# Moving the second expert item's first product ahead of the first item's down product

## The reference, cut to what matters

```python
gate = ...                      # [256, 32], two experts of one group of eight per token
h = silu(einsum('td,edf->tef', t, w1)) * einsum('td,edf->tef', t, w3)   # f = 512
h = h * gate[:, :, None]
y = einsum('tef,efd->td', h, w2)
out = rmsnorm(h_in + y)
```

## Time and profile before

| | us |
|---|---|
| median of 3 runs | 1465.17 (1464.26 to 1465.79) |
| the profiled execution | 1466.02 |
| its span in the trace | 1463.5 |
| TensorE busy | 1382.6 (94%) |
| VectorE busy | 553.4 (38%) |
| ScalarE busy | 341.1 (23%) |
| 16 DMA engines, large queue | 78.2% of the span |

### The profile page before, as it was taken

One profiled execution on the slowest core, in us unless ns is written; L12 is line 12 of the kernel. 1 busy time (PEld: TensorE's weight loads), 2 busy tenths in 40 slices (PEclk: granted clock), 3 DMA queues, 4 the chain that ended last, 5 costly groups with the idle time before them and its releaser, 6 DMA issues.

```text
span 1463.5 us, 19372 instructions
## 1 busy us (share of the span) xinstructions
PE 1382.6 (94%) x7304; PEld 784.6 (54%) x7304; DVE 553.4 (38%) x1103; ACT 341.1 (23%) x608; POOL 206.9 (14%) x195
## 2 busy tenths in 40 slices
PE   6999899998999999998999999899999999899896
PEld 5874698896687435433533543444534543443354
DVE  4899710424534423322313223223222332321345
ACT  3010158565565011110111111111121020121102
POOL 2000356676584000000000000000000000000000
PEclk9999999999999999999999999999999999999996
DMA  8433443344357599999999999959999999999991
GB/s 208 172 116 115 144 173 126 127 151 172 115 195 322 223 426 428 428 428 428 427 428 427 429 429 429 429 222 430 429 427 429 429 429 428 427 430 429 428 403 58
DMA packets 71374, 471.67 MB, mean 322 GB/s; under 512 B 17297, under 2 KB 17378, under 8 KB 46114
## 3 DMA queue, kind: packets, MB, share of 16 engines
q1 hardware_dynamic: 70674, 469.75, 78.2%
q10 hardware_dynamic: 528, 1.05, 0.2%
q0 software_dynamic: 128, 0.26, 0.1%
HBM read 468.95 MB, written 2.10 MB: 322 GB/s over the span
## 4 chain that ended last, share of the span: by engine, by line
PE 61%; DMA 19%; DVE 3%; ACT 1%; issue 1%; DVEq 0%; POOL 0%; POOLq 0%; ACTq 0%
PE ps L1767 24%; DMA ring<-in_expert_w_dram 19%; PE ps L1428 11%; PE ps L1785 11%; PE ps L1745 5%; PE ps L1775 3%; PE ps L1796 2%; PE ps L1797 2%; PE ps L1757 1%; PE ps L1717 1%; DVE reg_e L1074 0%; PE ps L1693 0%; DVE reg_y L1036 0%; DVE reg_x L1371 0%; PE ps L1551 0%
## 5 line engine op out<-in xcount | busy, mean ns | idle before, releaser
L1785 PE MATMUL ps<-ring,reg_y 128*64 128x512 f32 x1056 | 240.5, 609 | 8.7 <-DVE reg_y L1293 7.8
L529 POOL TENSOR_TENSOR w_lo<-ring,w_hi 128x512 fp32r<-128x512 f32 x144 | 185.3, 1316 | 87.5 <-ACT w_hi L586 86.1
L1299 DVE TENSOR_TENSOR y_lo_t<-ps,y_hi_t 64x512 fp32r<-64x512 f32 x132 | 90.9, 689 | 216.6 <-ACT y_hi_t L812 215.3
L1785 PEld LDWEIGHTS ps<-ring,reg_y 128*64 128x64 f32 x1056 | 75.4, 140 | 147.3 <-issue 143.6
L812 ACT ACTIVATE y_hi_t<-ps 64x512 fp32r<-64x512 f32 x132 | 78.0, 591 | 327.3 <-PE ps L1785 324.9
L1308 DVE TENSOR_TENSOR reg_x<-ps,reg_x 128x512 f32<-128x512 f32 x136 | 87.7, 684 | 131.1 <-PE ps L1797 131.1
L1767 PE MATMUL ps<-reg_e,reg_s 128*64 128x512 f32 x528 | 119.4, 594 | 10.6 <-POOLq L551 10.6
L1767 PE MATMUL ps<-ring,reg_s 128*64 128x512 f32 x528 | 120.0, 596 | 7.7 <-POOLq L551 7.2
L1767 PE MATMUL ps<-ring,reg_y 128*64 128x512 f32 x528 | 120.0, 596 | 6.8 <-POOLq L551 6.2
L1767 PE MATMUL ps<-reg_e,reg_y 128*64 128x512 f32 x528 | 119.3, 594 | 2.2 <-POOLq L551 1.4
L1288 DVE TENSOR_SCALAR reg_y<-ps,lamv 128x512 f32<-128x512 f32 x33 | 24.8, 751 | 242.9 <-PE ps L1767 242.9
(11 more groups left out here) (360 smaller groups left out, 1763.9 us busy)
## 6 DMA issues: line engine op xcount, KB each, us to landing
ring<-in_expert_w_dram SPq DMA_DIRECT2D x128, 2048.0 KB, 20.3
reg_e<-in_expert_w_dram SPq DMA_DIRECT2D x64, 2048.0 KB, 20.5
ring<-in_w_in_dram SPq DMA_DIRECT2D x20, 2048.0 KB, 7.9
ring<-in_w_out_dram SPq DMA_DIRECT2D x8, 2048.0 KB, 8.0
reg_x<-in_x_dram SPq DMA_DIRECT2D x4, 1024.0 KB, 8.6
out_dram<-reg_x SPq DMA_DIRECT2D x4, 512.0 KB, 2.7
reg_e<-in_ssm_w_glu_dram ACTq DMA_DIRECT2D x1, 1024.0 KB, 5.9
reg_e<-in_final_norm_g_dram SPq DMA_DIRECT2D x1, 1024.0 KB, 16.7
```

The lines of the kernel that those rows point to most:

```text
L529: G.tensor_tensor(w_lo[:, i % BUFS, :], unit(u % SLOTS_A)[:, c, :], w_hi[:, i % BUFS, :], ALU.subtract).then_inc(row_lo, 1)
L1299: last = V.tensor_tensor(y_lo_t[64 * q:64 * q + 64, w], psb[3 + k // 2][64 * (k % 2):64 * (k % 2) + 64, :], y_hi_t[64 * q:64 * q + 64, w], ...
L1785: last = M(psb[3 + i // 2][64 * (i % 2):64 * (i % 2) + 64, :], hT[:, 2 * half + f, :], unit2(s)[:, f, 512 * i:512 * i + 512], start=half = ...
```

## The change

In a pair, TensorE does the second item's w1 product before the first item's down product. ScalarE follows: it scales that product (`a_up`) before it takes out the first item's down product. The single semaphore `slot_free` becomes three, `free[0]`, `free[1]` and `free[2]` for w1, w3 and w2, as units are no longer released in the order in which they are loaded; each counts two units for an item. VectorE's order, SyncE's order of loads and POOL's order of counting stay.

```diff
-        def used(n_, k):
-            return n_ * 6 + SLOTS_B + k
+        def used(n_):
+            return n_ * 2 + 4
...
-        slot_free = sem("slot_free")
+        free = [sem(f"free{w}") for w in (1, 3, 2)]
...
                 for k in range(6):
                     s = slot_of(k)
-                    sp.wait_ge(slot_free, n_ * 6 + k + 1)
+                    sp.wait_ge(free[k // 2], n_ * 2 + k % 2 + 1)
...
             def a_items(i_, g_, n0, h, nq):
-                for q in range(nq):
-                    a_up(g_, n0 + q, QE * h + q)
-                    a.wait_ge(e_hT, n0 + q + 2)
-                    a_silu(n0 + q)
-                    a_down(i_, n0 + q, q)
+                a_up(g_, n0, QE * h)
+                a.wait_ge(e_hT, n0 + 2)
+                a_silu(n0)
+                if nq == 2:
+                    a_up(g_, n0 + 1, QE * h + 1)
+                a_down(i_, n0, 0)
+                if nq == 2:
+                    a.wait_ge(e_hT, n0 + 3)
+                    a_silu(n0 + 1)
+                    a_down(i_, n0 + 1, 1)
...
-                    last.then_inc(slot_free, 1)
+                    last.then_inc(free[m], 1)
...
-                    last.then_inc(slot_free, 1)
+                    last.then_inc(free[2], 1)
...
                 slots_to_rows(i_, h)
+                if nq == 2:
+                    up(n0 + 1, QE * h + 1, 0, (0, 1))
                 down(n0)
                 if nq == 2:
-                    up(n0 + 1, QE * h + 1, 0, (0, 1))
                     up(n0 + 1, QE * h + 1, 1, (0, 1))
                     turn(n0 + 1)
```

More of the change, by code:

```diff
@@ L466, in _ @@
                 item(sp.value_load(c_int[0:1, ds(e, 1)], min_val=1, max_val=ITEMS - 1), e)
-            sp.wait_ge(slot_free, (sp.value_load(n_extra[0:1, 0:1], min_val=0, max_val=EXTRA - 1) + NE) * 6 + 1)
+            sp.wait_ge(free[0], (sp.value_load(n_extra[0:1, 0:1], min_val=0, max_val=EXTRA - 1) + NE) * 2 + 1)
             sp.dma_start(fg, final_g.unsqueeze(0).broadcast_to([P, D])).then_inc(fg_in, 16)
@@ L801, in a_up @@
             def a_up(g_, n_, q):
-                a.wait_ge(slot_free, used(n_, 2))
+                a.wait_ge(free[0], used(n_))
                 a.wait_ge(e_hT, n_ + 1)
@@ L808, in a_down @@
             def a_down(i_, n_, q):
-                a.wait_ge(slot_free, used(n_, 6))
+                a.wait_ge(free[2], used(n_))
                 a.wait_ge(e_comb, i_ * 8 + 1)
@@ L1285, in v_up @@
             def v_up(n_, q):
-                v.wait_ge(slot_free, used(n_, 4))
+                v.wait_ge(free[1], used(n_))
                 v.wait_ge(e_hT, n_ + 1)
@@ L1652, in out_rows @@
                     if n_ >= len(OUT_UNITS) - SLOTS_A and i == 7:
-                        pe.sem_inc(slot_free, 1)
+                        pe.sem_inc(free[1], 1)
                     for b in range(TB):
@@ L1671, in _ @@
             pe.wait_ge(ny, 4)
-            pe.sem_inc(slot_free, 2)
+            pe.sem_inc(free[0], 2)
             def h_transpose(k):
@@ L1708, in _ @@
             pe.wait_ge(row_used, ROWS)
-            pe.sem_inc(slot_free, 2)
+            pe.sem_inc(free[2], 2)
             h_logits(2)
```

## The result

The kernel after the change takes 1503.4 us in the median of four runs (1498.2 to 1506.5), the kernel before it 1465.5 (1464.3 to 1466.3): a ratio of 1.0259 (95% interval 1.0242 to 1.0275), 37.9 us more. The forecast was 1492.0 in a range of 1476 to 1512, from a sum of 26.6 us more (on 1465.2 that makes 1491.8). The profiled execution took 1502.4 us with a span of 1500.7, so 37.2 us of span are to be accounted for.

A forecast was written before the change was run, and what follows sets the result against it. The prediction took the weight loads to bound the kernel. Start 9.0, hole 6.0, tail 3.9, loop 6.3 and clock 1.4 summed to 26.6 us over the 1465.2 median, giving 1492.0, range 1476 to 1512.

The forecast's parts named there:

- What bounds the kernel: Whole item stage: weight loads bound it, one 2 MB unit per 4.89 us; TensorE has 7.6 us spare every second pair.
- Start: First pair: moved w1 waits for VectorE's list of experts, so expert 1's w2a lands at 529.0, not 519.97; +9.0 us.
- Hole: The 12 us without loads at the shared expert's second pass: cut in two, not filled, item 18's w2 later; +6.0 us.
- Tail: After the last such pair: TensorE runs on its own work, 3.9 us later; +3.9 us.
- Loop: 14 regular pairs: second item's w2a, issued late, just catches its predecessor; 0 to 12.6 us, half taken, 6.3.
- Clock: TensorE idle 6.3 us in every second pair, 7 times, then at half clock; 1.4 to 12.6 us, 1.4 taken.
- Rival 1: Load queue deep enough, so only start and tail, or the tail alone, cost: 1469 to 1478; chance 0.09.
- Rival 2: Loop feeds on itself: clock costs 1.8 in each of 7 idle times, late load over 0.9 per pair; 1509 to 1525; chance 0.09.
- Rival 3: Faster at the hole: w1 of expert 17 issued up to 7.0 us earlier, before 973.3; about 1460; chance 0.04.
- Rival 4: No effect: order hidden under the loads, nothing of loop, start or tail; within 3 us; chance 0.03.

The follow-up runs named there:

- the kernel kept busy: Against the kernel after: seven unused 128x512 float32 products in TensorE's idle time in every second pair but the one behind the hole; 1506.1 us.
- the kernels that moved the release: On the kernel kept busy: w2a buffer released two or four products later, or half of down done inside w1b; 1503.0, 1513.8, 1489.7 us.

## Why the prediction was right, and where it was off

**What bounds the kernel** held. The loads do: where the rate went back to 427 (one w1 unit ahead; loads in the order of use) the loop cost nothing, also where TensorE waited up to 6.0 us. One sum of TensorE's work was slightly off: the terms given for a pair without a gather add to 50.8 and not 51.1, so the spare is 7.9 and not 7.6, which changes nothing.

**Start**, forecast 9.0, measured 9.2. w2a was to be issued at 521.7 and land at 529.0; it was issued at 521.6 and landed at 528.9. The step named VectorE's list as the cause, and making the list earlier took 6.6 of the 9.2 back; the old order in the first pair took back all of it.

**Hole**, 6.0 and 6.0. Expert 17's first load was to go out at 977.1 by the old clock; with 17.4 us of shift by then (w3b of expert 15 landed at 945.2 instead of 927.8) that is 994.5, and it went out at 995.79, 1.3 later. w3a went out at 1009.37, and the hole is cut in two, as forecast. The trace shows whose 1.3 us these are. First TensorE's row in before, then three rows of after, of which the last is the same product:

```profile
976.43 3.60 PE L1767 MATMUL ps<-reg_e,reg_y 128*64 128x512 f32 x16
...
930.59 6.20 PE L1772 MATMUL ps<-reg_e,reg_y 128*64 128x512 f32 x16 [6.55 <-POOLq L551]
936.62 3.60 PE L1772 MATMUL ps<-reg_e,reg_s 128*64 128x512 f32 x16
...
991.94 3.65 PE L1772 MATMUL ps<-reg_e,reg_y 128*64 128x512 f32 x16
```

SyncE issued 0.20 us after this product's end in both kernels (976.43 + 3.60 to 980.23, 991.94 + 3.65 to 995.79), so it was not late; TensorE was. In the pair ahead of the hole w1a ran at half clock for 6.20 us, and w1b started 1.2 us after its landing where the forecast had 0.1. That is 1.1 of the 1.3 us, a price of the clock that the forecast had taken as 0.2 per pair and put into the loop alone.

**Tail**, 3.9 and 4.1. Here too TensorE sets the time and not the loads. The last such pair had w1b 1.1 us after its landing, which lengthens the tail, and its w2a lost 0.9, which delays the last landing but not TensorE and so shortens the tail. The same pair of errors stands ahead of the hole (1.1 late, 1.0 lost at expert 15's w2a). That both terms came out at their numbers is in part luck: in the kernel kept busy nothing was late, the two w2a lost 2.5 and 2.3, and the hole cost 3.7 and the tail 2.0 us.

**Loop**, loads and clock, 7.7 against 17.1: this is the term that was mis-sized. Its mechanism was right in the main: half a unit of queue left, a load that just catches its predecessor, every later unit behind it. What it left out is that at such a lead the engines run dry for a moment and do not start again evenly, as shown for the kernel kept busy. I priced it at half of what the one nearest row gave, 0.9 at a lead of 3.0; the 13 loads lost 1.3 each. The reasoning behind the half (that the spacing of 12 units also held scatter) rested on one late unit in a full queue, 1.2 us at a lead of 20.5, which says nothing of a load that just catches its predecessor. And the bound of 0.9 each, taken as the upper one, was none, for a lead of 2.2 to 2.6 could lose up to 2.7. The lead in the sum was right (2.6: issued at t+7.2, the predecessor landing at t+9.8; measured 1.4 to 2.6); that such a lead is worse than a shorter one no row of before could show.

On this term the forecast weighed the Trainium skill (DMA: Bandwidth & Descriptors, Anatomy of one DMA), by which the fixed cost lies mostly in the receipt at the end. That section is on transfers issued by GpSimd, and these loads are SyncE's. By it a load issued over 2 us early would lose nothing. Thirteen leads of 2.5 to 2.8 lost 22.3 us, so the measurement decides against it here. The trace of before shows the split for the load issued at 980.23 on an empty queue, as two stretches and the packets from 986.6 to 987.3 us:

```profile
980.20:981.20 1.00, 1.00 (x8) 0.33 (x6) 0.00 (x0) 0.00 (x0) 0.00 (x0) 1.00 0.00 0
981.20:984.20 3.00, 3.00 (x18) 1.00 (x16) 0.00 (x0) 0.68 (x1) 0.00 (x0) 1.00 1.06 350
...
DMA packets 33, 0.28 MB, mean 398 GB/s; under 512 B 16, under 2 KB 16, under 8 KB 16
```

Nothing moves in the first 1.0 us, the rate is 350 and not 428 GB/s in the next 3, and the last of the 16 closing packets starts 0.3 us before the landing at 987.5. So most of what this load took beyond 4.9 us stands at its beginning and not at its end.

**Clock.** The idle times came as forecast, seven of 6.3 to 7.2 us (forecast 6.3), in every second pair, and the half clock followed, but for about 7 us and not for 3.3: four short rows near the code had been the wrong sample, since each stood behind a wait of 0.7 to 1.0 us and not of 7. Of the 1.4 to 2.6 us more that w1a took, up to 1.3 were spent while w1b was on its way; w1b then started late by 4.7 us in all in the seven pairs (forecast 1.4), 1.1 of it ahead of the hole and 1.0 ahead of the tail. Taking the slowness away won nothing in the total, as the longer leads lost more. Whether it would have been worth something had the loads not been worse at longer leads isn't separated.

**Rivals.** Rival 1 (queue deep enough, 1469 to 1478) fell: the 20 us on the page were a median, and the one load that mattered had a lead of 2. Rival 2 (1509 to 1525) had its first half, the idle 7 us at half clock, and a late load over 0.9 per pair, 1.3; it missed as the clock cost 0 to 1.1 us in a pair and not its 1.8. The time lies between its case and mine. The Trainium skill's page for it (TensorE: Matmul & The Clock Gate, HAM oscillation) describes the cold start that the trace shows here in every second pair, 5.0 to 6.2 us for a unit of 3.6; that it did not set the time is what the kernel kept busy showed. Rival 3 (faster) asked for an issue before 973.3; less the shift of 17.4 the kernel after has 978.4. Alone, its place gives 1.8 us, later lost. Rival 4 (no effect) fell.

## What to carry to other kernels

Before a product is moved ahead of the one that gives a buffer back, compare the order of use with the order in which the loads land, and count for the load behind that buffer how long ahead of its predecessor's landing it will be issued: here leads under 4 us cost time in nearly every place and leads of 4 to 5 us in some, and the median time to landing said nothing about that one load. Loads issued in order by one engine stand behind a held buffer even where their own is free, so a change of order at TensorE needs the same change at the queue, and then still breaks at each place where one item has no loads. Look at the first turn of the loop by itself: a wait that was covered by the moved work is paid there in full.

## What the hardware showed

- A 2 MB load on an empty queue landed 7.2 to 7.6 us after its issue in 53 of 65 places over all traces (the others up to 8.7); in a full queue one landed every 4.9 us. In before the load issued at 980.23 moved no data for 1.0 us, and its last closing packet started 0.3 us before its landing.
- The loss of a w2a load is not monotonic in its lead: 1.5 us at 0.9, 1.1 at 1.7 (13.7 / 13), 1.7 at 2.6 (22.3 / 13), 0.1 at 4.2, none from 4.9 on. Eight w2b loads with leads of 3.9 to 4.2 lost 0.3 to 1.5 all the same.
- A load lands 0.3 to 0.5 us after the last of its 16 closing packets in nearly all cases. If these are one for each DMA engine, a load lands with its slowest engine. At leads of 2.5 to 2.8 half of them had ended 0.9 to 3.3 us before the landing, and the loss went with that time; at a lead of 1.0 all 16 ended within 0.7 us of each other. In a full queue half of them can be 2.2 us ahead too (before), and no time is lost. Why some fall behind is open, and the mean DMA share of 0.99 over 117 us hides both this and the short dry stretches.
- Single units in bursts of issues lose 0.4 to 1.5 us at odd places, one in before too (1.2); they grew to 7 to 10 us in all in the kernels that moved the release. Also open.
- SyncE's pause between the last load of one expert and the first of the next was 1.4 us in after (525.34 to 526.73) and 0.4 us between two loads of one (527.06 to 527.46). It costs nothing where SyncE waits for a buffer anyway, as in the hole. Its cause wasn't tried.
- In and after an idle time of about 7 us TensorE's granted clock was at half (0.51, the level of 1.2 GHz) for 6.8 us, once for 10.2. In the stretch from 567.0 to 573.9 us 2.3 of the 6.9 us still lay in the idle time.
